# Two bias rows per matmul: the gate and up biases of an expert kernel taken as pairs of 64-row matmuls at the head of each accumulation

## What is computed

```python
def expert_block(args):
    xe, e = args
    gate = jnp.minimum(xe @ w_gate[e] + b_gate[e], SWIGLU_LIMIT)
    up = jnp.clip(xe @ w_up[e] + b_up[e], -SWIGLU_LIMIT, SWIGLU_LIMIT)
    act = (up + 1) * (gate * jax.nn.sigmoid(SWIGLU_ALPHA * gate))
    return act @ w_down[e] + b_down[e]

yb = lax.map(expert_block, (xb, block_e)).reshape(-1, h.shape[-1])
```

## Time and profile before

| | |
|---|---|
| median of 3 runs | 3129.93 us (3125.41 to 3139.72) |
| span of the profiled execution | 3128.4 us |
| its own time | not told apart in the list of runs; the nearest of the three is 3129.93 us, 1.5 us above the span |
| PE busy | 2940.3 us, 94% of the span |
| DVE / ACT busy | 2055.0 / 1580.6 us |
| first and last bias matmul | 1833.9 and 3057.3 us from the start |

### The profile page before, as it was taken

How to read it: one execution, slowest core, us unless ns; L and a number is a source line. 1 busy time by engine, 2 the same in 40 slices (tenths; PEclk the granted TensorE clock), 3 DMA queues, 4 the chain that set the end, 5 groups by cost and what they waited for, 6 DMA issues and landing times. The chain is left out here.

```text
span 3128.4 us, 41852 instructions
## 1 busy us (share of the span) xinstructions
PE 2940.3 (94%) x15092; PEld 2339.7 (75%) x15092; DVE 2055.0 (66%) x2444; ACT 1580.6 (51%) x1697; POOL 440.5 (14%) x409
## 2 busy tenths in 40 slices
PE   6989999996999999889999779999999999999996
PEld 3668888764687888766677768888888888888883
DVE  8451223658732235745752489999999999999994
ACT  4242222334632224434532267777777777777771
POOL 1002100011212100003100011111221121111211
PEclk9899999997999999999999789999999999999997
DMA  6512222211022222110022469999999999999983
GB/s 243 217 69 84 105 102 100 85 59 52 15 108 105 98 108 88 54 68 1 1 78 84 178 236 385 388 380 384 388 387 385 378 385 388 386 387 376 386 342 143
DMA packets 86861, 641.54 MB, mean 205 GB/s; under 512 B 9792, under 2 KB 10240, under 8 KB 23456
## 3 DMA queue, kind: packets, MB, share of 16 engines
q1 hardware_dynamic: 76144, 601.61, 49.8%
q0 software_dynamic: 10224, 37.23, 3.1%
q10 hardware_dynamic: 384, 1.19, 0.1%
HBM read 616.36 MB, written 23.63 MB: 205 GB/s over the span
## 5 line engine op out<-in xcount | busy, mean ns | idle before, releaser
L2940 DVE TENSOR_TENSOR arena_rounded<-arena,arena_rounded 128x2048 fp32r<-128x2048 f32 x420 | 951.1, 2285 | 93.8 <-ACT arena_rounded L2936 93.8
L2936 ACT ACTIVATE arena_rounded<-arena 128x2048 fp32r<-128x2048 f32 x420 | 801.7, 1918 | 211.6 <-PE banks L263 139.3
L261 PE MATMUL banks<-arena_rounded,operand_rounded 128*128 128x512 f32 (+1 forms) x2064 | 819.9, 397 | 5.9 <-DVE operand_rounded L2932 3.0
L262 PE MATMUL banks<-arena_rounded,operand_rounded 128*128 128x512 f32 (+1 forms) x2064 | 803.5, 389 | 0.0
L263 PE MATMUL banks<-arena_rounded,operand_rounded 128*128 128x512 f32 (+1 forms) x1504 | 584.9, 389 | 0.0
L261 PEld LDWEIGHTS banks<-arena_rounded,operand_rounded 128*128 128x128 f32 x2064 | 390.2, 189 | 84.4 <-issue 7.5
L262 PEld LDWEIGHTS banks<-arena_rounded,operand_rounded 128*128 128x128 f32 x2064 | 390.3, 189 | 78.1 <-issue 1.0
L263 PEld LDWEIGHTS banks<-arena_rounded,operand_rounded 128*128 128x128 f32 x1504 | 284.1, 189 | 59.1
L261 PE MATMUL banks<-operand_rounded,arena_rounded 128*128 128x512 f32 (+2 forms) x712 | 267.9, 376 | 6.0 <-PE banks L263 5.2
L262 PE MATMUL banks<-arena_rounded,arena_rounded 128*128 128x512 f32 (+1 forms) x688 | 266.8, 388 | 0.0
L263 PE MATMUL banks<-operand_rounded,arena_rounded 128*128 128x512 f32 (+2 forms) x712 | 264.5, 372 | 0.0
(11 more groups left out here) (477 smaller groups left out, 3807.3 us busy)
## 6 DMA issues: line engine op xcount, KB each, us to landing
arena<-in_gate SPq DMA_DIRECT2D x140, 1024.0 KB, 6.5
arena<-in_up SPq DMA_DIRECT2D x140, 1024.0 KB, 7.0
arena<-in_down SPq DMA_DIRECT2D x140, 1024.0 KB, 5.7
arena<-in_dense SPq DMA_DIRECT2D x62, 2048.0 KB, 7.6
arena<-routed SPq DMA_DIRECT2D x4, 2048.0 KB, 14.4
arena<-in_dense SPq DMA_DIRECT2D x6, 1024.0 KB, 5.0
small<-in_rows SPq DMA_DIRECT2D x7, 512.0 KB, 7.6
resid<-in_x SPq DMA_DIRECT2D x4, 512.0 KB, 6.7
```

The costliest lines, as they stand in the source:

```text
L261: nc.tensor.matmul(out, left[0], right[0], start=start, stop=False)
L262: nc.tensor.matmul(out, left[0], right[1], start=False, stop=False)
L2936: nc.scalar.activation(high[q % NHI], raw[:, q, :], ACT.Copy).then_inc(high_ready, 1)
L2940: nc.vector.tensor_tensor(low[q], raw[:, q, :], high[q % NHI].bitcast(F32), ALU.subtract).then_inc(low_ready, 1)
```

## The change

Nothing but the biases is touched. The bias tile becomes 1024 columns wide: rows 0 to 63 hold the gate biases (high, low), rows 64 to 127 the up biases (high, low). The constant `pick` has ones in all four groups of 32 rows. Each bias matmul takes 64 rows: gate from rows 0 to 63 into bank 2h, up from rows 64 to 127 into bank 2h + 1. The two stand side by side at the head of q = 0 and of q = 4, where they start both accumulations; the four matmuls of line 3017 go.

```diff
-    e["bias_raw"] = w[:, at - PIECE:at]
-    e["bias"] = piece_at(PIECES + NHI)
+    e["bias_raw"] = w[:, at - PIECE:at - PIECE + D]
+    e["bias"] = piece_at(PIECES + NHI)[:, 0:D]
...
-            for n in range(2):
-                act.dma_start(e["bias_raw"][n * NE:(n + 1) * NE, :], k.io["moe_bias"]).then_inc(bias_in, 16)
+            for n in range(4):
+                role = slice((n // 2) * D, (n // 2 + 1) * D)
+                act.dma_start(e["bias_raw"][n * NE:(n + 1) * NE, :], k.io["moe_bias"][:, role]).then_inc(bias_in, 16)
...
-            low = slice(NE, 2 * NE)
-            V.tensor_tensor(e["bias"][low, :], e["bias_raw"][low, :], e["bias"][low, :].bitcast(F32), ALU.subtract)
+            for low in (slice(NE, 2 * NE), slice(3 * NE, 4 * NE)):
+                V.tensor_tensor(e["bias"][low, :], e["bias_raw"][low, :], e["bias"][low, :].bitcast(F32), ALU.subtract)
...
-            nc.gpsimd.memset(e["bias_raw"][2 * NE:, :], 0.0).then_inc(bias_zero, 1)
-            pool.wait_ge(bias_in, 32)
-            up_bias = e["bias_raw"][0:2 * NE, D:2 * D]
-            nc.gpsimd.tensor_scalar(up_bias, up_bias, 1.0, None, ALU.add).then_inc(bias_zero, 1)
+            pool.wait_ge(bias_in, 64)
+            up_bias = e["bias_raw"][2 * NE:4 * NE, :]
+            nc.gpsimd.tensor_scalar(up_bias, up_bias, 1.0, None, ALU.add).then_inc(bias_up, 1)
...
+            def add_biases(b, h):
+                if h == 0:
+                    pe.wait_ge(chosen, b + 1)
+                for role in range(2):
+                    rows = slice(2 * NE * role, 2 * NE * (role + 1))
+                    nc.tensor.matmul(k.psum[:, 2 * h + role, :], e["choice"][rows, :], half(e["bias"], h)[rows, :], start=True, stop=False)
+
...
                     for q in range(PIECES):
                         pe.wait_ge(low_ready, PIECES * b + (q + 1))
+                        if q in (0, 4):
+                            add_biases(b, q // 4)
...
-                                i = exact_product(nc, k.psum[:, r, :], x, (w[0][:, j, :], w[1][:, j, :]), start=(d == 0), stop=False)
-                            if q % 2 == 1:
-                                if q == 1:
-                                    pe.wait_ge(chosen, b + 1)
-                                at = (r % 2) * D + (r // 2) * NB
-                                i = nc.tensor.matmul(k.psum[:, r, :], e["choice"], e["bias"][:, at:at + NB], start=False, stop=True)
+                                i = exact_product(nc, k.psum[:, r, :], x, (w[0][:, j, :], w[1][:, j, :]), start=False, stop=(d == DT - 1))
...
-    put("pick", (i[:, None] % NE == np.arange(NE)) & (i[:, None] < 2 * NE))
+    put("pick", i[:, None] % NE == np.arange(NE))
```

More of the change, by code:

```diff
@@ L2726, in route @@
     names = ("logits", "chain", "exp", "member", "ranked", "counted", "marked", "entered",
-             "spread", "spread_turned", "rows_out", "turned_back", "copied", "bias_in", "bias_zero", "bias_split")
-    (logits_s, chain, exped, member_s, ranked, counted, marked, entered, spread_s, spread_turned, rows_out, turned_back, copied, bias_in, bias_zero, bias_split) = (k.sem(f"route_{n}") for n in names)
+             "spread", "spread_turned", "rows_out", "turned_back", "copied", "bias_in", "bias_up", "bias_split")
+    (logits_s, chain, exped, member_s, ranked, counted, marked, entered, spread_s, spread_turned, rows_out, turned_back, copied, bias_in, bias_up, bias_split) = (k.sem(f"route_{n}") for n in names)
     with nc.Block() as block:
@@ L2747, in _ @@
                                      ACT.Copy).then_inc(copied, 1)
-            act.wait_ge(bias_in, 32)
-            act.wait_ge(bias_zero, 2)
+            act.wait_ge(bias_in, 64)
+            act.wait_ge(bias_up, 1)
             nc.scalar.activation(e["bias"], e["bias_raw"], ACT.Copy).then_inc(bias_split, 1)
```

## The result

The changed kernel takes 3145.5 us (median of 12 runs, 3140.6 to 3155.3) against 3129.7 us for the kernel before (12 runs); the ratio is 1.0045, with a 95% interval of 1.0034 to 1.0057. By the ratio that is 14 us more, between 10.6 and 17.8; the two medians lie 15.8 us apart, and the spans of the two profiled executions 13.3 us. Forecast were 3141.7 us and +11.8.

What follows compares the result with a forecast made beforehand. PE's matmul stream was taken to bound the expert loop; pairs 11.2, feeders 0.5 and `route` 0.1 us sum to +11.8 us, giving 3141.7 us against the median. The forecast range was +6 to +15 us, chance 0.60.

Steps and rivals of the forecast that it cites:

- What a bias costs now: PE's stream in the expert loop: each full bias matmul takes 0.245 us; removing four saves 0.98 us a block.
- What a pair costs: Two 64-row matmuls at once: 0.65 us from edges, loads, columns and late starts, read from plain float32 attention rows.
- the entry: Between the last 128-row matmul and the 64-row pair: PE is empty for 0.10 us.
- the exit: Between the end of the 64-row pair's streaming and the next group: PE is empty for 0.10 us.
- The worry that fp32r might differ from plain float32: Pair cost came from plain float32 attention rows; the forecast is wrong if fp32r edges differ in either direction.
- +0.16 us a pair, +11.2 us: Expert loop: a 0.65 us pair replaces two biases of 0.49 us; two pairs a block, 70 pairs.
- Feeders: DVE's slack to PE around q = 10 shrinks to 0.04 to 0.07 us; 0.5 us for all blocks, bounds 0 and 3.5.
- `chosen`: PE's wait for POOL's choice moves from q = 1 to q = 0, 2.7 us earlier; 10 us to spare, no cost.
- `route`: Preparation before the loop: DVE's 2048-column subtraction becomes two of 1024, +0.1 us on the path; ACT's gain hidden.

Runs made afterwards that it cites:

- e5: Changed kernel without any gate and up bias matmuls, that part of the computation left out; period 34.65 us, one time of 3102.4 us.
- e6: Changed kernel with both pairs in one stretch at the head of q = 0 and the feeders reordered earlier; 3127.4 us, ratio to before 0.9992.
- e8: Changed kernel with the feeders reordered earlier (second hidden half turned after q = 8); period 35.81 us, ratio to before 1.0052.
- e9: Kernel before with the feeders reordered earlier, as the control; period 35.475 us, ratio to before 1.0005.
- e1: Kernel before with its four full 128-row biases moved to the heads of q = 0 and q = 4, two at each; period 35.675 us, ratio to before 1.0029.

## Why the prediction was right, point by point

**What a bias costs now.** Taken at 0.245 us, 0.98 us a block. e5 and before differ by 0.815 us; with the 0.08 us that e5 loses at q = 0 and some 0.05 at q = 10, as the changed kernel, that is 0.945 us, 0.236 a bias. The term holds within 0.04 us a block.

**What a pair costs.** Taken at 0.65 us from the attention rows, measured at 0.64. Each part can be worked out from a distance of starts now: the entry 0.32 - 0.227 = 0.09 us, the exposed load of the pair 0.34 - 0.227 = 0.11 us (e6, from pair to pair), the exit 0.32 - 0.227 = 0.10 us (e6, from the second pair to the product), the exposed load of the next product 0.33 - 0.227 = 0.10 us. The worry that fp32r might differ from plain float32 was groundless. A second weak point wasn't seen: in the earlier trace rows the matmuls ahead of the 64-row pair are of the form 128*64, pairs on two halves of the columns, and not the full 128*128 of the expert loop. So the entry was read from another border than the one it was used for; that the two agree, 0.10 and 0.09 us, was luck as far as the prediction goes.

The Trainium skill, TensorEngine Tiling (Array Packing), § Tiling Modes, says that a change of the tiling mode drains the engine. The trace agrees, with the 0.09 and 0.10 us at the two sides of a stretch. The Trainium skill, TensorE: Matmul & The Clock Gate, § Part 3: Packing small matmuls, says that a weight load on another group of rows overlaps with running matmuls. The trace agrees inside a stretch: the two matmuls of a pair start 0.003 us apart, each with its own load. It doesn't show this across the edges, where the pair's loads start with their matmuls, 0.32 us behind the last product.

**+0.16 us a pair, +11.2 us.** Measured at 0.17 (e8 against e9), 0.335 x 35 = 11.7 us.

**Feeders.** The step named the right place at q = 10 and a slack that was a little too large. It left 0.07 us between DVE's end and the weight load there, while 0.12 us pass between the two where PE does wait (2432.30 and 2432.42); the difference is the 0.05 us by which the product is late. It was put at 0.5 us for all blocks and is 0.04 us a block, 1.4 to 1.6 us, inside its bounds of 0 and 3.5. This is the term of the sum that was most off, by some 1 us. What it missed is that the same chain of DVE ends a third time, at `x_ready` for the head of the next block. In the changed kernel the entry's empty stretch hides it, so the sum was right in spite of the gap; in e1, where nothing hides it, it was 0.16 us a block with the wait for `chosen` behind it, and my expectation for e1 fell with it.

**`chosen`.** The wait moves from the end of q = 1 to the head of q = 0. That is 24 products, 5.45 us earlier, and not the 2.7 us of the prediction, whose own 2431.4 and 2436.86 say so; the 10 us to spare stand. POOL's write isn't waited for in any run, and in the changed kernel the wait costs nothing, as said. That PE's program must still pass it, which seems to have cost e1 0.08 us, wasn't thought of.

**`route`.** Put at +0.1 us; the two subtractions of 1024 columns take 2.45 us instead of 2.28, here in DVE's timeline of the changed kernel:

```profile
1810.75 2.45 DVE L2881 TENSOR_TENSOR arena_rounded<-arena,arena_rounded 32x1024 fp32r<-32x1024 f32 x2
```

That is +0.17 us on the path. ACT's copy fell to 1.06 us, hidden as said.

**The first block.** It costs 1.4 us more, of which 0.4 are what every block pays: from its row transposes at 1821.3 us to the next at 1858.3 are 37.0 us, against 35.6 before (1822.0 to 1857.6). This is PE's timeline there in the changed kernel:

```profile
1826.32 0.79 PE L3006 MATMUL banks<-arena_rounded 64*128 64x512 f32 x2 [3.14 <-DVE operand_rounded L2932]
...
1831.47 0.63 PE L262 MATMUL banks<-arena_rounded,operand_rounded 128*128 128x512 f32 x1
1831.90 0.52 PE L263 MATMUL banks<-arena_rounded,operand_rounded 128*128 128x512 f32 x1
```

From 1825 to 1830 us the granted clock is 0.50 here, its lower level, 1.2 GHz, after 3.1 us in which PE waited for DVE. The spacing of 0.43 us lasts until 1831.9, 5.6 us after the first matmul; before, it lasted from 1826.96 until 1829.7, 2.7 us. The pair isn't what delays the rise. In e5, which has no bias matmul at all, the same spacing lasts 6.1 us (1826.21 to 1832.34), in e8, with the same pairs, 4.3 us (1828.53 to 1832.84), and in e9, whose stream on PE there is that of before, 4.4 us. So it falls otherwise from one profiled execution to the next, and the 1 us of it in the difference of the two spans is chance, as far as these traces show.

**The account of the span**: 34 blocks +13.1, the first block +1.4, the loop's start -0.7 (1821.3 against 1822.0, other stages), what follows the last transposes -0.5 (63.7 against 64.2 us): +13.3 us, which is 3141.7 - 3128.4. The steady part alone, 0.385 us over 35 blocks, is 13.5 us, against the 11.7 us of the prediction's pairs and feeders. So the mechanism was right and each term is a little short: 0.5 us in the pairs, some 1 us in the feeders. That the rest of the span adds almost nothing (1 us in the first block against 1.2 us less ahead of it and at the end) is chance. Of the prediction's "+6 to +15 us" the result is at the upper end: 14 us by the ratio, 13.3 by the spans, 15.8 by the medians. The interval of the ratio, 0.34% to 0.57%, has the half per cent of its chances inside it.

## What to carry to other kernels

Halving the number of passes of a small-row matmul is worth nothing if each group of them stands alone in a stream of full ones: a stretch of 64-row matmuls cost 0.41 us beyond its columns here (two edges, two exposed loads), as much as 1.8 full matmuls of 512 columns, so put all such matmuls of an iteration side by side or leave them full. With four biases a block even one stretch only broke even: its time can't be told from that of the kernel before. The price could be read beforehand from another stage of the same program that mixes both shapes. And when a matmul is taken out of a stream that bounds the kernel, list every point at which the feeders' chain meets it again, with the semaphore's time taken off the slack.

## What the runs showed of the hardware

- A single 64-row fp32r matmul between 128-row ones occupies PE for as long as a pair on both row halves (0.32 + 0.42 + 0.34 against 0.32 + 0.43 + 0.33 us): the second half is free, at the full rate of 512 columns in 0.23 us, though both write PSUM at once.
- Weight loads are exposed across the border of a stretch, 0.11 us for 64 rows and 0.10 to 0.11 for 128. Inside the 64-row stretch only the loads of the first pair (0.11 of its 0.34 us, e6) cost anything; those of the second don't, and the product comes 0.32 us behind it.
- Where DVE releases PE after the last product before the wait has started, the loss isn't DVE's lateness alone. DVE ended 0.07 to 0.08 us after the start of the last product in e5 and in e1, and PE lost 0.08 and 0.16 us. From DVE's end to the weight load that waits for it passed 0.12 us in e5 and at q = 10 of the changed kernel, and 0.21 us in e1, where one more semaphore that had long been set is waited for in between. None of this appears in the list of waits, because the modelled end of the previous matmul covers it; it shows in the distance of starts.
